# Sliding attention moved between the input projections of the first block, with an output projection by halves of rows and norm sums with tokens on partitions

## The chip, the cores and the metric

The kernel runs on one core of a Trainium2 chip. The metric is the device time of one execution in microseconds. The core has TensorE (PE in the rows, its weight loads PEld), VectorE (DVE), ScalarE (ACT), GpSimd (POOL) and SyncE (SP). They work through instruction streams of their own and meet at semaphores.

## The reference

Three transformer blocks on 256 tokens of width 1024 in float32. The change touches the mixer of the first one:

```python
mod = c_act @ w_ada[l] + b_ada[l]
shift1, scale1, gate1, shift2, scale2, gate2 = jnp.split(mod, 6, axis=-1)
h = modulate(x, norm1_g[l], shift1, scale1)
proj = h @ w_in[l]
q_g, k_g, v_g, a_lr, r_g, q_s, k_s, v_s = jnp.split(proj, split_at, axis=-1)
...
o_gla = rms_norm(o_gla, gla_norm_g[l].reshape(GLA_HEADS, GLA_DV)).reshape(bsz, s, GLA_WIDTH)
o_gla = o_gla * jax.nn.silu(r_g)
o_swa = swa_mixer(...)
o_swa = rms_norm(o_swa, swa_norm_g[l])
y = jnp.concatenate([o_gla, o_swa], axis=-1) @ w_out[l]
x = x + gate1[:, None, :] * y
h2 = modulate(x, norm2_g[l], shift2, scale2)
x = x + gate2[:, None, :] * peer_mixer(h2, ...)
```

`gla_mixer` is a gated linear attention in chunks of 64 tokens with 4 heads. `swa_mixer` is attention over a window of 128 keys with 8 query heads, 2 key heads and a sink logit per head. `peer_mixer` picks 16 of 128 x 128 experts per head and token. Two more blocks follow, with a sparse and a compressed attention; the change leaves them alone.

## The kernel before, in words

Everything is kept transposed: features on the 128 partitions, the 256 tokens along the row, a vector of width 1024 as 8 chunks. Weights come from HBM as 488 slots of 128x1024 float32 through a ring of four, in one fixed order (`_COUNTS`); SyncE refills a ring place as soon as `slots_used` says that it is free. Each engine's order is written out by hand in its block, and a projection result passes through one of two banks of `pu` (`entry`), freed by `evacs`.

*Front.* GpSimd issues 16 DMAs for the first rows of `w_ada` (the modulation). VectorE takes the dot product of each row with silu(c) (`modulation`), the squares of x are summed over features by matmuls with an all-ones matrix (`norm_sum`), which leaves the same sum in all 128 partitions, ScalarE takes the root, VectorE the reciprocal of 128x256, and scales x into `HTf`. Before the reciprocal VectorE waits for six small DMAs (`small_loaded`) to copy a table of position biases, which TensorE spreads in eight matmuls (line 724). A low-rank product (line 729) gives the gate logits.

*Projections.* 18 slots of `w_in` in the order qg, kg, rg, qs, ks, vg, vs; the first 13 by `project` (line 555, 8 matmuls of 256 columns), five by `project_tokens` (line 567, 16 of 128). ScalarE copies each result out (rg through Silu). A float32 matmul is two passes in the trace. Beside them VectorE takes the cumulated gates and 18 of the remaining 32 modulation rows, which come through a ring of four rows (`aring`) that GpSimd refills in a loop (line 444), one row for each row used.

*Gla.* After the last projection ScalarE makes five exponentials, VectorE seven products (lines 1690 to 1695), and TensorE scores (line 755), transposes, states, inner and outer products (to line 788). The norm over each head's 128 features sums into `pm` and `pn` and takes the reciprocal of 128x1024 (line 1730).

*Sliding attention.* `attend("swa", ...)` has 16 units, one per head and block of 128 tokens: the 8 of the first block have 128 keys, the others 256. In step u, TensorE does the scores of unit u (line 666) into one of four banks, the transposition of unit u-3 (line 675) and the products of unit u-4 (line 702); VectorE adds bias, takes the maximum and normalizes, ScalarE exponentiates and copies. Eight modulation rows are fillers of VectorE there. Then comes its norm, again through `norm_sum`.

*Output projection.* Each of 8 slots of `w_out` gives 128 output features from all 8 chunks of the input (`up_slot`). Products here and later are made of three passes (`three`, lines 587 to 589), with the weights and the input split into a high and a low part: ScalarE writes `ring_hi` (line 368), VectorE or GpSimd subtracts to get `ring_lo` (line 375); the same for the input, `Xh` and `Xl` (`x_high`, `x_low`). VectorE adds the residual. ScalarE squares each chunk, GpSimd adds the squares (`h2sum`).

*Second norm and peer query.* Root, reciprocal, scaling, high and low parts of eight chunks (lines 1804, 1810), then 16 slots of `peer_q`, whose low parts are GpSimd's; after each, `key_scores` (line 842) and VectorE's selection of the best 16. GpSimd fills most of the large buffer `big` with ones for a later stage: its middle, where gla's tensors lay (`mid_lo` to `mid_hi`, line 449, after `gla_done`), and the rest (lines 451 and 452). `aring` lies in `big` too. From here on, 128 slots of `peer_u` and all that follows are the same in both kernels.

## Time and profile before

| | |
|---|---|
| median of 3 runs | 1766.5 us (1765.46 to 1768.02) |
| profiled execution | 1767.21 us, span 1765.6 us |
| PE busy | 1650.5 us, 93% of the span |
| DVE, ACT, POOL busy | 1078.7, 855.1, 487.9 us |
| granted TensorE clock, mean | 0.951 |

The span runs from the first to the last instruction of the profiled execution. Busy shares are means over stages that have different limits, so what one stage costs is read from stretches of the timeline. The granted clock is a share of 2.4 GHz and has two levels, 0.5 and 1.0; a value between is a mean over time.

### The profile page before, as it was taken

To read this page: it belongs to the slowest core of one execution; us is meant where nothing else is said; L and a number is where in the kernel's file an instruction comes from. 1 tells how busy PE (TensorE), PEld (TensorE's weight loads), DVE (VectorE), ACT (ScalarE), POOL (GpSimd) and SP (SyncE) were. 2 spreads that over 40 slices of the span, in tenths; PEclk is the share of its full clock that TensorE was granted. 3 is DMA by queue.
4 is the path that set the end of the run, shared out by engine and by line. 5 is a ranking of instruction groups with operands and counts; after the bars stand their busy time and mean duration, and the time that the engine had idled before them with its cause. 6 is when DMAs were issued, how large, how long until landed. Compare 5 with 4: busy or idle time off the path is not lost.

```text
span 1765.6 us, 33664 instructions
## 1 busy us (share of the span) xinstructions
PE 1650.5 (93%) x11072; PEld 1492.8 (85%) x11072; DVE 1078.7 (61%) x2455; ACT 855.1 (48%) x1808; POOL 487.9 (28%) x465
## 2 busy tenths in 40 slices
PE   5975889998999999999999999889999998899998
PEld 2773689998999999987888887779999988789997
DVE  5536558953777771355555555866555665755555
ACT  3213445555454444555555554265555535654554
POOL 3110456986666668500000001320000000310000
PEclk8985699999999999999999999889999999999999
DMA  8861144554443445555555555215555456045554
GB/s 309 312 226 57 39 138 144 170 178 140 143 140 134 142 143 169 182 192 192 192 190 190 190 190 178 78 58 165 181 181 185 147 176 205 25 144 175 185 187 155
DMA packets 81329, 288.17 MB, mean 163 GB/s; under 512 B 10144, under 2 KB 11472, under 8 KB 81136
## 3 DMA queue, kind: packets, MB, share of 16 engines
q1 hardware_dynamic: 72448, 257.30, 44.6%
q0 software_dynamic: 7488, 26.87, 4.1%
q10 hardware_dynamic: 1328, 3.15, 0.5%
q8 instruction: 39, 0.64, 0.1%
q14 instruction: 26, 0.21, 0.0%
HBM read 284.66 MB, written 2.62 MB: 163 GB/s over the span
## 4 chain that ended last, share of the span: by engine, by line
PE 83%; DVE 8%; ACT 3%; issue 2%; DMA 2%; POOL 1%; SPq 0%; DVEq 0%; ACTq 0%; POOLq 0%
PE pu L587 12%; PE pu L588 12%; PE pu L589 12%; PE pacc L646 8%; PE pacc L644 8%; PE pacc L645 8%; PE pu L555 3%; PE pu L567 2%; PE pacc L587 2%; PE pacc L589 2%; PE pacc L588 2%; PE pacc L702 2%; PE pm L874 2%; PE pn L874 2%; DVE ring_lo L375 1%
## 5 line engine op out<-in xcount | busy, mean ns | idle before, releaser
L368 ACT ACTIVATE ring_hi<-ring 128x512 fp32r<-128x512 f32 x912 | 524.2, 622 | 546.7 <-PE pu L589 290.5
L375 DVE TENSOR_TENSOR ring_lo<-ring,ring_hi 128x512 fp32r<-128x512 f32 x624 | 407.4, 695 | 356.5 <-ACT ring_hi L368 356.1
L587 PE MATMUL pu<-Xh,ring_hi 128*128 128x256 f32 x1472 | 432.5, 294 | 21.6 <-DVE stats L1756 4.3
L588 PE MATMUL pu<-Xl,ring_hi 128*128 128x256 f32 x1472 | 420.1, 285 | 0.0
L589 PE MATMUL pu<-Xh,ring_lo 128*128 128x256 f32 x1472 | 420.0, 285 | 0.0
L375 POOL TENSOR_TENSOR ring_lo<-ring,ring_hi 128x512 fp32r<-128x512 f32 x288 | 370.3, 1307 | 131.4 <-ACT ring_hi L368 130.8
L587 PEld LDWEIGHTS pu<-Xh,ring_hi 128*128 128x128 f32 x1472 | 285.9, 194 | 28.8 <-issue 15.7
L588 PEld LDWEIGHTS pu<-Xl,ring_hi 128*128 128x128 f32 x1472 | 286.5, 195 | 0.2
L589 PEld LDWEIGHTS pu<-Xh,ring_lo 128*128 128x128 f32 x1472 | 285.8, 194 | 0.0
L644 PE MATMUL pacc<-ring_hi,vh 128*128 128x512 f32 x512 | 200.5, 392 | 0.0
L646 PE MATMUL pacc<-ring_lo,vh 128*128 128x512 f32 x512 | 200.5, 392 | 0.0
L645 PE MATMUL pacc<-ring_hi,vl 128*128 128x512 f32 x512 | 199.8, 390 | 0.0
L587 PE MATMUL pu<-X2h,ring_hi 128*128 128x256 f32 x512 | 146.3, 286 | 3.2 <-DVE big L2088 3.2
L589 PE MATMUL pu<-X2h,ring_lo 128*128 128x256 f32 x512 | 145.6, 284 | 0.0
L588 PE MATMUL pu<-X2l,ring_hi 128*128 128x256 f32 x512 | 145.6, 284 | 0.0
L644 PEld LDWEIGHTS pacc<-ring_hi,vh 128*128 128x128 f32 x512 | 96.0, 187 | 33.2 <-issue 5.6
L646 PEld LDWEIGHTS pacc<-ring_lo,vh 128*128 128x128 f32 x512 | 96.1, 188 | 21.0
L645 PEld LDWEIGHTS pacc<-ring_hi,vl 128*128 128x128 f32 x512 | 96.2, 188 | 16.0
L473 POOL DMA_DIRECT2D big<-bias_row x8 | 4.3, 549 | 363.1 <-DVE stats L1999 363.1
L587 PEld LDWEIGHTS pu<-X2h,ring_hi 128*128 128x128 f32 x512 | 99.0, 193 | 4.2 <-DVE big L2088 3.6
L588 PEld LDWEIGHTS pu<-X2l,ring_hi 128*128 128x128 f32 x512 | 98.9, 193 | 0.3
L589 PEld LDWEIGHTS pu<-X2h,ring_lo 128*128 128x128 f32 x512 | 99.0, 193 | 0.0
(390 smaller groups left out, 2653.1 us busy)
## 6 DMA issues: line engine op xcount, KB each, us to landing
ring<-in_weights SPq DMA_DIRECT2D x488, 512.0 KB, 3.3
big<-in_ada POOLq DMA_DIRECT2D x40, 512.0 KB, 6.7
bias_row<-big ACTq DMA_DIRECT2D x1, 1536.0 KB, 6.9
XT<-in_xT ACTq DMA_DIRECT2D x1, 1024.0 KB, 8.2
scr<-in_ada POOLq DMA_DIRECT2D x2, 512.0 KB, 12.3
tk<-in_ada POOLq DMA_DIRECT2D x2, 512.0 KB, 14.0
early_h<-in_ada POOLq DMA_DIRECT2D x2, 512.0 KB, 16.0
early_l<-in_ada POOLq DMA_DIRECT2D x2, 512.0 KB, 17.6
```

Of the source, the lines that this page charges most:

```text
L368: nc.scalar.activation(ring_hi[:, n % 2, half], ring[:, n % RING, half], ACT.Copy).then_inc(s["split_hi"], 1)
L375: api.tensor_tensor(ring_lo[:, n % RING, half], ring[:, n % RING, half], ring_hi[:, n % 2, half], ALU.subtract).then_inc(s[LOW[name][0]], 1)
L555: last = mm(entry(e), slot(n)[:, c * P:(c + 1) * P], rhs[:, c, :], start=(c == 0), stop=(c == C - 1))
L567: last = mm(entry(e)[:, tt * P:(tt + 1) * P], lhs[:, c, tt * P:(tt + 1) * P], slot(n)[:, c * P:(c + 1) * P], start=(c == 0), stop=(c == C ...
L587: mm(out, ring_hi[:, n % 2, w], xh, start=start, stop=False, skip_group_check=True)
L588: mm(out, ring_hi[:, n % 2, w], xl, start=False, stop=False, skip_group_check=True)
L589: return mm(out, ring_lo[:, n % RING, w], xh, start=False, stop=stop, skip_group_check=True)
L644: mm(out, xh[:, rows], ring_hi[:, n % 2, w], start=False, stop=False, skip_group_check=True)
L645: mm(out, xl[:, rows], ring_hi[:, n % 2, w], start=False, stop=False, skip_group_check=True)
L646: last = mm(out, xh[:, rows], ring_lo[:, n % RING, w], start=False, stop=False, skip_group_check=True)
L702: last = mm(out, v, p, start=(kind != "nsa" and k == 0 and UNITS[u][4]), stop=(k == len(pairs) - 1 and UNITS[u][5]), skip_group_check=(kin ...
L874: last = mm((pm, pn)[k % 2][:, i * P:(i + 1) * P], sq[:, j // 2, j % 2 * P:(j % 2 + 1) * P], scr[:, j * P:(j + 1) * P], start=True, stop=True)
```

## The change

- *Order of the weights.* `w_in` comes as qs, ks, vs, qg, kg, vg, rg. `w_out` comes as four slots for the attention's 512 input features and four for gla's; each slot gives 256 output features from four input chunks (`halves_of`, `out_slot`), so each output chunk gets two residuals, and each residual has two halves.
- *Attention among projections.* `attend` may return one step as a function. After projection 6 + k, TensorE does the steps that `steps_after(k, 20)` names, one or two. ScalarE follows the same table after each copy out. Scores use two banks (`pm`, `pn`) in place of four. VectorE's fillers there are one modulation row per step and, from step 8, the seven gla products. The gla exponentials stand after copy 5 on ScalarE. Silu of rg is one operation later on.
- *Sums with tokens on partitions.* For the norms of the input, the attention and gla, the squares are the stationary operand and one column of ones moves, so 128 tokens come out as a column of 128 partitions. Root and reciprocal are 128x2 or 128x8. A matmul of the column, repeated 128 times (`over_columns`), with the identity spreads it over all partitions again (`spreads`), and VectorE reads it from PSUM. The second norm keeps the old form.
- *Waits.* The bias table has a semaphore for its own two DMAs (`relb_loaded`). GpSimd's two long memsets become 14 of at most 128x1024, one after each low part of `peer_q`; ahead of the first low part GpSimd waits for `ada_used` to reach 48, all rows. VectorE takes modulation rows 40 to 43 in the output projection and 44 to 47 after the second norm.

```diff
+EARLY, BESIDE = 6, 12
...
+def steps_after(k, total):
+
+    return range(k * total // BESIDE, (k + 1) * total // BESIDE)
+
+
+NORMS = ["n1", "swa", "gla", "n2", "fin", "attn0", "lat", "mlp0", "attn1", "mlp1", "fin2"]
...
+        def over_columns(col):
+
+            return bass.AP(tensor=col.tensor, offset=col.offset, ap=[list(col.ap[0]), [0, P]])
+
+        def score_psum(u, banks=4):
+            return (pm[:, 0:T], pn[:, 0:T], pu[:, 0, 0:T], pu[:, 1, 0:T])[u % banks]
...
-            for dst, src, sem in ((cols[:, :], cols_d, "cols_loaded"), (relb[0:NB, :], relb_d, "small_loaded"),
-                                  (oneh[0:NB, :], onehot_d, "small_loaded"), (walr, small_d[:, :, 0:16], "small_loaded"),
+            for dst, src, sem in ((cols[:, :], cols_d, "cols_loaded"), (relb[0:NB, :], relb_d, "relb_loaded"),
+                                  (oneh[0:NB, :], onehot_d, "relb_loaded"), (walr, small_d[:, :, 0:16], "small_loaded"),
...
-            pool.wait_ge(s["x_split"], 2 * XSPLIT["w_out"] + 2)
-            step(nc.gpsimd.memset(big[:, GATED_FROM:mid_lo, :], 1.0))
-            nc.gpsimd.memset(big[:, mid_hi:NKEY, :], 1.0).then_inc(s["ones_set"], 1)
...
-            for c in range(2, C - 1):
...
             last.then_inc(s["h2_sum"], 1)
             pool.wait_ge(s["slots_used"], SLOT["peer_q"])
+            pool.wait_ge(s["x_split"], 2 * XSPLIT["w_out"] + 2)
+            pool.wait_ge(s["ada_used"], MOD)
+            parts = [(k, min(k + 4, hi)) for lo, hi in ((GATED_FROM, mid_lo), (mid_hi, NKEY)) for k in range(lo, hi, 4)]
             for i in range(2 * PH):
                 split_low(pool, nc.gpsimd, "peer_q", i)
+                for lo, hi in parts[i::2 * PH]:
+                    step(nc.gpsimd.memset(big[:, lo:hi, :], 1.0))
+            nc.gpsimd.memset(ones_flag, 1.0).then_inc(s["ones_set"], 1)
...
+                banks = 2 if kind == "swa" else 4
...
                 def scores(u):
-                    if u >= 4:
-                        pe.wait_ge(s["att_biased"], u - 3)
-                    mm(score_psum(u)[:, 0:keys_of(u)], query(u), keys(u), start=True, stop=True)\
+                    if u >= banks:
+                        pe.wait_ge(s["att_biased"], u + 1 - banks)
+                    mm(score_psum(u, banks)[:, 0:keys_of(u)], query(u), keys(u), start=True, stop=True)\
                         .then_inc(s["att_scored"], 1)
...
-            norm_sum("n1")
-            pe.wait_ge(s["small_loaded"], 16 * 6)
+            pe.wait_ge(s["squares"], SQUARED["n1"])
+            for tt in range(TT):
+                for c in range(C):
+                    last = mm(pn[:, tt:tt + 1], sq[:, c, tt * P:(tt + 1) * P], ones[:, 0:1], start=(c == 0), stop=(c == C - 1))
+            last.then_inc(s["sums"], 1)
+            pe.wait_ge(s["consts_made"], 1)
+            pe.wait_ge(s["inverses"], 1)
+            for tt in range(TT):
+                last = mm(pm[:, tt * P:(tt + 1) * P], over_columns(R[:, tt:tt + 1]), ident[:, :], start=True, stop=True)
+            last.then_inc(s["spreads"], 1)
+            pe.wait_ge(s["relb_loaded"], 16 * 2)
...
+            for i in range(18):
+                if i == 5 or 10 <= i < 14:
+                    project_tokens(SLOT["w_in"] + i, USE["w_in"] + i, HTf)
+                else:
+                    project(SLOT["w_in"] + i, USE["w_in"] + i, HTf)
...
+                if i == EARLY:
+                    pe.wait_ge(s["la_parts"], 1)
+                    pe.wait_ge(s["evacs"], USE["w_in"] + EARLY)
+                if i >= EARLY:
+                    for step in steps_after(i - EARLY, swa_steps):
+                        swa_step(SPAN["swa"][0] + step)
...
+            pe.wait_ge(s["squares"], SQUARED["swa"])
+            for tt in range(TT):
+                for c in range(4):
+                    last = mm(paccf[:, tt:tt + 1], sq[:, c, tt * P:(tt + 1) * P], ones[:, 0:1], start=(c == 0), stop=(c == 3))
+            last.then_inc(s["sums"], 1)
...
+            pe.wait_ge(s["inverses"], 2)
+            for tt in range(TT):
+                last = mm(paccf[:, tt * P:(tt + 1) * P], over_columns(R[:, tt:tt + 1]), ident[:, :], start=True, stop=True)
+            last.then_inc(s["spreads"], 1)
...
+            def out_slot(i):
...
+                pe.wait_ge(s["evacs"], e - 1)
+                if i % 4 == 0:
+                    pe.wait_ge(s["x_split"], 2 * XSPLIT["w_out"] + i // 4 + 1)
+                for j in range(2):
+                    for c in range(4):
+                        if j == 0 and c % 2 == 0:
+                            split_ready("w_out", i, c // 2, None)
+                        last = three(pu[:, e % 2, j * T:(j + 1) * T], n, slice(c * T + j * P, c * T + (j + 1) * P),
+                                     Xh[:, x0 + c, :], Xl[:, x0 + c, :], c == 0, c == 3)
+                last.then_inc(s["slots_used"], 1)
...
+            out_slot(0)
...
-            for i in range(C):
-                up_slot("w_out", i, USE["w_out"] + i, None, 0, "w_out" if i == 0 else None)
...
+            for h in range(GH):
+                for tt in range(TT):
+                    last = mm(paccf[:, h * TT + tt:h * TT + tt + 1], sq[:, h, tt * P:(tt + 1) * P], ones[:, 0:1], start=True, stop=True)
+            last.then_inc(s["sums"], 1)
+            out_slot(1)
+            pe.wait_ge(s["inverses"], 3)
+            for h in range(GH):
+                for tt in range(TT):
+                    col = 8 + h * TT + tt
+                    last = mm((pm, pn)[h // 2][:, (h % 2 * TT + tt) * P:(h % 2 * TT + tt + 1) * P], over_columns(R[:, col:col + 1]),
+                              ident[:, :], start=True, stop=True)
+            last.then_inc(s["spreads"], 1)
+            for i in range(2, 8):
+                out_slot(i)
+
...
+            act.wait_ge(s["sums"], NORM["n1"])
+            f(R[:, 0:TT], pn[:, 0:TT], ACT.Sqrt, scale=1.0 / D, bias=eps[:, 0:1]).then_inc(s["roots"], 1)
...
+                    evac(n_slot, rs[:, i - 14, :], src)
+                if i == EARLY - 1:
+                    act.wait_ge(s["ex_ready"], 1)
+                    inv = 1.0 / GATE_TEMP
...
+                    act.wait_ge(s["row_stored"], 16)
+                if i >= EARLY:
+                    for st in steps_after(i - EARLY, swa_steps):
+                        swa_step(SPAN["swa"][0] + st)
+            swa_step(SPAN["swa"][1] + 4)
...
+            squares(os_, sq[:, 0:4, :])
...
+            act.wait_ge(s["sums"], NORM["swa"])
+            f(R[:, 0:TT], paccf[:, 0:TT], ACT.Sqrt, scale=1.0 / 512, bias=eps[:, 0:1]).then_inc(s["roots"], 1)
+            split_high(act, "w_out", 0)
...
+            split_high(act, "w_out", 1)
+            act.wait_ge(s["evacs"], USE["w_in"] + 18)
+            f(rs, rs, ACT.Silu).then_inc(s["silu_done"], 1)
+            act.wait_ge(s["normed"], NORM["swa"])
+            x_high(os_, 0)
...
+            x_high(og, 1)
+            for i in range(3, 6):
...
+            for i in range(4, C - 1):
+                if i + 2 < C:
+                    split_high(act, "w_out", i + 2)
+                else:
+                    split_high(act, "peer_q", i + 2 - C)
+                act.wait_ge(s["evacs"], USE["w_out"] + i + 1)
+                for c in (2 * i - 8, 2 * i - 7):
+                    f(sq[:, c, :], XT[:, c, :], ACT.Square).then_inc(s["h2_sq"], 1)
...
-            dve.wait_ge(s["small_loaded"], 16 * 6)
-            v.tensor_copy(relb_all[0:NB, :, :], strided(relb[0:NB, 0:1], [[1, NH], [0, P]])).then_inc(s["relb_spread"], 1)
+            modulation(0, 4)
             dve.wait_ge(s["roots"], NORM["n1"])
-            step(v.reciprocal(R[:, 0:T], R[:, 0:T]))
+            v.reciprocal(R[:, 0:TT], R[:, 0:TT]).then_inc(s["inverses"], 1)
+            modulation(4, 2)
+            dve.wait_ge(s["spreads"], 1)
             for c in range(C):
-                last = v.scalar_tensor_tensor(HTf[:, c, :], XT[:, c, :], column("n1", c), R[:, 0:T], ALU.mult, ALU.mult)
+                last = v.scalar_tensor_tensor(HTf[:, c, :], XT[:, c, :], column("n1", c), pm[:, 0:T], ALU.mult, ALU.mult)
...
+            modulation(2 * C, 6)
...
+            def swa_filler(i):
+
+                modulation(2 * C + 6 + i, 1)
+                if 8 <= i < 8 + 3 + NSUB:
+                    gla_product(i - 8)
+
+            dve.wait_ge(s["consts_made"], 1)
+            dve.wait_ge(s["small_loaded"], 16 * 4)
+            attend("swa", swa_bias, filler=swa_filler)
...
+            for i in range(4):
+                last = v.scalar_tensor_tensor(os_[:, i, :], os_[:, i, :], column("swa_g", i), paccf[:, 0:T], ALU.mult, ALU.mult)
+            last.then_inc(s["normed"], 1)
+            split_low(dve, v, "w_out", 0)
...
+            x_low("w_out", os_, 0)
+            split_low(dve, v, "w_out", 1)
+            dve.wait_ge(s["ada_used"], 2 * C + 24)
+            step(v.tensor_tensor(mod[:, 16:40], mod[:, 16:40], cols[:, COL["b_ada"] + 16:COL["b_ada"] + 40], ALU.add))
+            step(v.tensor_scalar(gain[:, 8:16], mod[:, 32:40], 1.0, None, ALU.add))
+            step(v.tensor_tensor(gain[:, 8:16], gain[:, 8:16], cols[:, COL["n2"]:COL["n2"] + 8], ALU.mult))
+            modulation(2 * C + 24, 1)
...
+            v.reciprocal(R[:, 8:8 + GH * TT], R[:, 8:8 + GH * TT]).then_inc(s["inverses"], 1)
...
+            def out_residual(i):
+
+                e = USE["w_out"] + i
+                dve.wait_ge(s["slots_used"], SLOT["w_out"] + i + 1)
+                for j in range(2):
+                    o = 2 * (i % 4) + j
+                    last = v.scalar_tensor_tensor(XT[:, o, :], pu[:, e % 2, j * T:(j + 1) * T], mod[:, 16 + o:17 + o], XT[:, o, :],
+                                                  ALU.mult, ALU.add)
+                last.then_inc(s["evacs"], 1)
...
+            out_residual(0)
+            modulation(2 * C + 25, 1)
+            dve.wait_ge(s["spreads"], 3)
...
+            dve.wait_ge(s["silu_done"], 1)
             v.tensor_tensor(og, og, rs, ALU.mult).then_inc(s["gla_done"], 1)
...
+            split_low(dve, v, "w_out", 2)
+            out_residual(1)
+            x_low("w_out", og, 1)
+            for i in range(2, C):
+                if i + 1 < C:
+                    split_low(dve, v, "w_out", i + 1)
+                out_residual(i)
+                if i < 4:
+                    modulation(2 * C + 24 + i, 1)
+            rest = 2 * C + 28
...
+            modulation(rest, MOD - rest)
+            dve.wait_ge(s["ada_used"], MOD)
+            step(v.tensor_tensor(mod[:, 40:48], mod[:, 40:48], cols[:, COL["b_ada"] + 40:COL["b_ada"] + 48], ALU.add))
...
-        tiles(np.concatenate([qg, kg, rg, qs, ks, vg, vs], axis=1)), tiles(w_out),
+        tiles(np.concatenate([qs, ks, vs, qg, kg, vg, rg], axis=1)), halves_of(w_out[512:]), halves_of(w_out[:512]),
```

The order of TensorE among the projections (`pu` holds projections, `pm` and `pn` scores, `pacc` transpositions and products; L555, L567 and from now L571, L583 are projections). Before:

```order
L555 MATMUL pu<-big,ring 128x256 x8
L737 MATMUL pn<-big 128x256 x2
L555 MATMUL pu<-big,ring 128x256 x96
L567 MATMUL pu<-ring,big 128x128 x80
L755 MATMUL pm<-big 64x16 x16
```

With the change, from projections 1 to 4 on:

```order
L571 MATMUL pu<-big,ring 128x256 x32
L583 MATMUL pu<-ring,big 128x128 x16
L571 MATMUL pu<-big,ring 128x256 x8
L684 MATMUL pm<-big 128x128
L571 MATMUL pu<-big,ring 128x256 x8
L684 MATMUL pn<-big 128x128
L684 MATMUL pm<-big 128x128
L571 MATMUL pu<-big,ring 128x256 x8
L684 MATMUL pn<-big 128x128
L693 MATMUL pacc<-ident,big 128x128
L684 MATMUL pm<-big 128x128
L693 MATMUL pacc<-ident,big 128x128
```

One or two units' pieces now stand behind each projection, and the gla scores (L755) come behind all of them.

The order of GpSimd from the loop of modulation rows to the low parts of the peer query, with the semaphores it waits on. Before:

```order
L444 DMA big<-in_ada 128x1024
L440 REGISTER_ALU
L440 COMPARE_AND_BRANCH
L449 MEMSET big 128x1024 [waits gla_done]
L449 MEMSET big 128x1024 [waits chain_pool] x7
L449 MEMSET big 128x512 [waits chain_pool]
L451 MEMSET big 128x5632 [waits x_split,chain_pool]
L452 MEMSET big 128x8192 [waits chain_pool]
L455 TENSOR_TENSOR R<-sq 128x256 [waits h2_sq]
L458 TENSOR_TENSOR R<-R,sq 128x256 [waits h2_sq,chain_pool] x5
L375 TENSOR_TENSOR ring_lo<-ring,ring_hi 128x512 [waits split_hi,slots_used]
L375 TENSOR_TENSOR ring_lo<-ring,ring_hi 128x512 [waits split_hi] x31
```

With the change:

```order
L462 MEMSET big 128x1024 [waits gla_done]
L462 MEMSET big 128x1024 [waits chain_pool] x7
L462 MEMSET big 128x512 [waits chain_pool]
L465 TENSOR_TENSOR R<-sq 128x256 [waits h2_sq,chain_pool]
L468 TENSOR_TENSOR R<-R,sq 128x256 [waits h2_sq,chain_pool] x4
L388 TENSOR_TENSOR ring_lo<-ring,ring_hi 128x512 [waits ada_used,split_hi,x_split,slots_used]
L388 TENSOR_TENSOR ring_lo<-ring,ring_hi 128x512 [waits split_hi]
L479 MEMSET big 128x1024
L388 TENSOR_TENSOR ring_lo<-ring,ring_hi 128x512 [waits split_hi,chain_pool]
```

The long memsets are gone from ahead of the sum of squares, a piece stands behind each two halves of a low part, and the first low part has `ada_used` among its waits.

## Rows read from the trace of the kernel before

**Rows 1.** Busy time by stretches: start:end and length, PE, PEld, DVE, ACT, POOL busy, clock, DMA.
```profile
42.10:112.40 70.30, 67.55 (x373) 60.11 (x372) 28.75 (x46) 13.33 (x27) 9.52 (x18) 0.95 0.83 309
112.40:122.06 9.66, 0.00 (x1) 0.01 (x1) 4.36 (x8) 5.24 (x7) 0.00 (x0) 0.76 0.18 54
122.06:140.03 17.97, 17.28 (x212) 16.51 (x212) 9.30 (x19) 1.68 (x3) 3.17 (x6) 0.50 0.53 177
...
147.55:163.50 15.95, 1.23 (x8) 0.93 (x8) 14.65 (x20) 5.39 (x10) 0.00 (x0) 0.50 0.00 0
163.50:197.60 34.10, 32.83 (x96) 17.19 (x96) 27.55 (x91) 15.68 (x61) 10.34 (x13) 0.52 0.19 62
...
206.80:232.90 26.10, 26.10 (x193) 25.91 (x194) 12.51 (x20) 11.73 (x22) 16.14 (x8) 0.88 0.45 138
232.90:244.90 12.00, 6.54 (x28) 5.03 (x26) 9.24 (x20) 5.89 (x12) 4.93 (x4) 0.72 0.17 54
248.70:295.00 46.30, 46.30 (x393) 46.30 (x392) 34.81 (x204) 22.25 (x54) 33.23 (x27) 1.00 0.48 160
```

**Rows 2.** Timeline of ScalarE in the projections: start, us, what [idle before <-releaser].
```profile
84.17 0.38 ACT L1168 ACTIVATE big<-pu 128x256 f32<-128x256 f32 x1 [3.07 <-PE pu L555]
```

**Rows 3.** Chain of waits, first 160 us: start, length, piece.
```profile
5.91 16.66 DMA sinks<-in_sinks
22.60 0.68 DVE big L1647
23.28 1.67 DVE R L1649
24.98 3.25 DVE big L1651 x8
...
147.55 6.57 DVE big L1730
```

**Rows 4.** Timelines of ScalarE and VectorE: the first root, a modulation row, an attention bias.
```profile
17.07 0.47 ACT L1168 ACTIVATE R<-pn,eps 128x256 f32<-128x256 f32 x1 [4.20 <-PE pn L577]
...
18.14 1.22 DVE L1638 CUSTOM_DVE_ANT_0 scr<-scr,big 128x1024 f32<-128x1024 f32 x1
...
184.95 0.41 DVE L1743 SCALAR_TENSOR_TENSOR big<-big,pn 128x256 f32<-128x256 f32 x1
```

**Rows 5.** Waits from 240 to 480 us: who waited for whom, total, times, longest.
```profile
DVE scr L1896 <- ACT tk L1168: 43.6, 1, 43.6
```

**Rows 6.** Chain of waits in the sliding attention, a unit with 256 keys.
```profile
183.69 1.15 PE pn L666 x2
184.84 0.62 PE pacc L675 x2
185.46 1.05 PE pacc L702 x4
```

**Rows 7.** The last block's attention: TensorE's timeline, and the stretch (columns as rows 1).
```profile
1520.23 0.27 PE L675 MATMUL pacc<-ident,big 128*128 128x128 f32 x1
1520.34 0.61 PE L702 MATMUL pacc<-big 128*128 128x128 f32 x4
...
1521.22 0.27 PE L675 MATMUL pacc<-ident,big 128*128 128x128 f32 x1
...
1520.00:1525.00 5.00, 5.00 (x37) 4.36 (x36) 4.23 (x16) 4.13 (x18) 2.38 (x5) 1.00 0.01 3
```

**Rows 8.** The same view as rows 1: the first 6.3 us of the output projection.
```profile
206.80:213.10 6.30, 6.30 (x30) 6.30 (x31) 1.28 (x2) 1.75 (x3) 3.89 (x1) 0.51 0.00 0
```

**Rows 9.** Timeline of GpSimd: memsets, and low parts of the peer query's weights.
```profile
175.27 8.69 POOL L449 MEMSET big<- 128x1024 f32 x9
...
233.11 4.93 POOL L375 TENSOR_TENSOR ring_lo<-ring,ring_hi 128x512 fp32r<-128x512 f32 x4 [0.52 <-PE pu L589]
```

**Rows 10.** Chain of waits in the second norm: the root.
```profile
235.37 0.48 ACT R L1168
```

205 lines of the change are left out of this document (91 added, 114 removed).

## Prediction

> **What bounds the kernel now.** I read four views of the trace before: the busy time by stretches, the chain of waits, the timelines of single engines, and the waits. The stretches [rows 1] show two kinds of stage. In the input projections (42.1 to 112.4 us), the output projection (206.8 to 232.9) and everything from 248.7 on, TensorE is busy throughout; each projection tile takes 3.45 us (0.38 of ScalarE's copy and 3.07 of its wait), a little more in the token form [rows 2]. Between 112.4 and 206.8 us TensorE either idles or works at a granted clock of about 0.5, the 1.2 GHz level. It waits 9.7 us for exponentials and gla products, works 18.0 us on gla, idles nearly all of 147.6 to 163.5, then spends 34.1 us on sliding attention. In the chain [rows 3] a reciprocal of 128x1024 alone costs 6.57 us. At the front, the chain runs through the DMA of the sinks into a small copy at 22.60, and only then to the reciprocal for the first norm, though the root was ready at 17.54 [rows 4]. So what the change moves lies on the path to the end, up to the first peer query; behind that TensorE is the bound, and VectorE, which would be late next, sits 43.6 us waiting on ScalarE [rows 5]. A gain at the front should therefore reach the end whole.
>
> **The change, part by part.** I follow the kernel by the moments at which stages begin. All differences are after minus before.
>
> 1. Front. The copy of the bias table now waits for its own two small DMAs, and the sums with tokens on partitions make the reciprocal 128x2 instead of 1.67 us wide. The two dot products that end at 19.4, 1.22 each [rows 4], become the last thing ahead of the scaling, which starts at 19.6 instead of 24.98 [rows 3]. All later modulation rows were there without a wait, so the first projection moves from 42.1 to 36.7: **-5.4** (bounds -3, if late rows of DMA hold it, and -6).
>
> 2. Projections and attention together. TensorE's own work adds up. At the half clock a unit with 256 keys is 1.15 + 0.62 + 1.05 = 2.8 us [rows 6], and the whole stage 34.1 [rows 1]. The attention of the last block does the same kind of steps at clock 1.00: a step of one transposition, four products and a 256-wide score repeats every 0.99 us [rows 7]. At those rates (0.11 per 128-wide pass, 0.22 per 256-wide one) eight short units are 8 x 0.56 and eight long ones 8 x 1.11, together 13.4. Half of 34.1 is 17. I take **+16** (bounds 13.4, and 20 with small waits). Cover: a step needs 2.2 us of VectorE for 128 keys and 3.1 for 256 keys (0.41 of bias, about as much of maximum, 0.5 of reciprocal and scaling, 0.1 of copy, 1.22 of a modulation row [rows 4], 0.6 of a gla product), while TensorE, with 12 projections and 16 us over 20 steps, comes round every 2.9 us. VectorE thus holds the pace, with little to spare in the second half. ScalarE's five gla exponentials (5.2 us busy with their table load, [rows 1]) lie beside projections 6 and 7.
>
> 3. The gap of 9.7 us ahead of the gla scores goes, for gla's products are done in VectorE's fillers: **-9.7**.
>
> 4. Gla. Before: 18.0 us at clock 0.50. Added are 16 one-column passes for the attention's sums and 4 passes that spread the roots, 2.5 us at 0.11 to 0.13 each; a gain is that the stage now follows dense work, so its first few us should run at the full clock. I take 17.5: **-0.5** (bounds -9, all of it at full clock, and +3).
>
> 5. From the last gla product to the end of the output projection. Before: 140.0 to 232.9 is 92.9 us. After, counted from that product: VectorE adds (1.0), ScalarE has Silu's table load and 1.1 for x_high, x_low takes 1.2, so slot 0 starts at 2.9. Its 24 passes run at the half clock, 6.30 us for 30 [rows 8], to 8.1; sums 1.5; slot 1 2.9; the gla spread 16 x 0.11, to 14.8. Then TensorE has nothing: four scalings 1.7, the product with rs 1.2 and the first half of slot 2's low part 0.6 stand ahead, to 18.4. Slots 3, 4 and 5 start each 3.2 apart, since VectorE puts two half splits (1.2), two residuals (0.8) and a modulation row or x_low (1.2) between them; slots 5, 6 and 7 take 2.9 each. End: 36.7. Difference **-56.1** (bounds -60 and -51).
>
> 6. The second norm. Before: 12.0. The last residual is two outputs wide (+0.8 with its square). GpSimd is now late: it leaves its loop of modulation DMAs only when row 43 is used, 27.4 in the count of step 5, then does nine memsets in 8.7 us [rows 9] and five additions of 0.8, so its sum arrives 4.0 after the last slot. Three matmuls, 1.7 in all, then the old 9.5 from root to last low part (235.4 to 244.9) [rows 1, 10]: 15.2, **+3.2** (bounds 0.8 and 5).
>
> 7. The wait for all modulation rows. The freed region holds the ring of rows, so GpSimd may not start peer_q's low parts before row 47 is used, and VectorE uses the last four after the norm: 4 x 1.15 = 4.6. Queued behind that wait are the low parts of slots 0 and 1, which before were done at 233 to 238, ahead of need [rows 9]. TensorE starts 1.3 after the rows, 5.9 from the norm's end, on a cold clock: slot 0 5.1, slot 1 3.4, scores 0.45, so slot 2 begins 14.8 after the norm instead of 3.8: **+11.0** (bounds 5, at full clock, and 14).
>
> 8. Memsets among the splits. Each of 14 slots of peer_q gets 0.9 more on GpSimd: 2.5 (4.93 for two slots) + 0.95 = 3.5 against TensorE's 3.3, the 46.3 us of 14 slots [rows 1, 9]. That loses 0.2 a slot, 2.5 in all, and the low parts are about as far ahead: **0** (bounds 0 and +4). The two long memsets that they replace were off the path and return nothing. VectorE's selection may be slowed by them, and is covered by its 43.6 us.
>
> Sum: -5.4 + 16 - 9.7 - 0.5 - 56.1 + 3.2 + 11.0 = **-41.5 us**. The profiled execution took 1767.2 us (span 1765.6), the median is 1766.5, 0.7 lower. 1766.5 - 41.5 = **1725 us**.
>
> **Rivals.**
> A. *The clock falls among the projections* (slower). Each burst of attention has short waits and transpositions. If TensorE's clock goes to 0.5 at project 7 and stays, 12 tiles go from 3.45 to 6.8 each (+40) and attention from 16 to 34 (+18): 1725 + 58 = 1783 us. The result changes sign when the half clock holds over some 41 of these 58, 70% of the stage. For it: the old attention kept TensorE busy for 32.8 of 34.1 us, and the granted clock was 0.52 in the mean [rows 1]. Against it: the last block's attention stood at 1.00, as from 1520 to 1525 [rows 7], and here dense tiles lie between the bursts. I give 5%. The Trainium skill, in "TensorE: Matmul & The Clock Gate", section "A second HAM failure mode: psum-queue depth-cycling", says that short idle moments between matmul groups that cycle through PSUM banks are frequent enough to make the clock swing between its levels; this kernel now cycles two score banks. By that rule the sum would lie near this rival, or halfway to it; by the row of the last block the clock stays. The row decides for me.
> B. *The attention's chain is exposed at every step.* With two score banks in place of four, a step waits on the bias of the one before the last, and VectorE's 3.1 us in the second half may exceed TensorE's round. Ten steps late by 1 us give +10, 1735 us; chains exposed by 1.5 us in all 16 units give +24, 1749 us. For it: VectorE's 3.1 against 2.9. Against it: units lie one whole projection apart. 15%.
> C. *Gla and slot 0 at the full clock*, since dense work goes ahead: -9 and -2, 1714 us. Against it: gla ran at 0.50 through 64-wide products and never raised the clock [rows 1]. 12%.
> D. *Little of it shows*, because VectorE or GpSimd, not TensorE, ends what comes after (peer_q at GpSimd's 3.5 or worse, the selection past its 43.6 us): +15 to +40, up to 1765 us. 5%.
>
> **How the numbers follow.** My forecast, the sum with its sizes off by up to 10, gets 63%; A 5%, B 15%, C 12%, D 5%. The range leaves out A, D and the far part of B: **1712 to 1745 us**. No change within 0.2% (3.5 us, about what these runs can tell) is only an edge of D and of A's partial form: 1%. Slower: A, 4%. Faster: 95%.
>
> **What would show it.** In the profile after: VectorE's first scaling near 19.6 us; the first projection near 37; clock 1.0 from 55 to 120 us, with attention's passes 0.11 and 0.22 long; gla scores starting near 123; output projection from about 143 to 177 with a hole of 3 to 4 us after slot 1; nine memsets ending near 177 and TensorE waiting on GpSimd's sum; VectorE's four dot products between the norm and GpSimd's first peer_q split, with TensorE idle for some 6 us there; then slots of peer_q at 3.3 to 3.5. Steps 2, 5 and 7 carry the sum: step 2 is wrong if the clock row falls among the projections, 5 if slots 2 to 7 take over 22 us, 7 if the first peer query starts without GpSimd's wait.

## The result, and the profile after

The changed kernel takes **1737.6 us** (median of 4 runs, 1736.7 to 1738.2) against 1766.3 for the kernel before beside it (4 runs, 1765.5 to 1768.0): a ratio of 0.985, 95% interval 0.983 to 0.987, or 28.7 us less. 1725 was forecast, 1712 to 1745 was the range. The profiled execution took 1736.7 us (span 1735.0, granted clock 0.971 in the mean; before 1765.6 and 0.951).

The stretches of the trace after answer to [rows 1]. The cuts are the starts of the scaling, of the first projection, of project 6, of the gla scores, of the second part of gla, the end of gla, slot 0 of the output projection and its end, root and end of the second norm, the first peer query and its slot 2. Columns as there.

```profile
21.31:38.39 17.08, 15.16 (x33) 6.01 (x31) 15.74 (x39) 8.07 (x16) 2.13 (x4) 1.00 0.87 333
38.39:65.15 26.76, 24.04 (x117) 20.53 (x117) 12.71 (x20) 7.46 (x13) 2.64 (x5) 0.94 0.72 261
65.15:129.91 64.76, 64.42 (x363) 50.24 (x361) 43.93 (x125) 26.64 (x82) 10.05 (x19) 1.00 0.80 278
129.91:134.40 4.49, 4.49 (x130) 4.46 (x129) 0.00 (x0) 1.33 (x2) 0.00 (x0) 1.00 0.28 103
134.40:148.30 13.90, 13.89 (x105) 13.02 (x104) 5.42 (x14) 7.50 (x11) 0.00 (x0) 0.51 0.00 1
148.30:150.75 2.45, 0.00 (x0) 0.03 (x1) 2.35 (x4) 2.43 (x4) 0.00 (x0) 0.50 0.00 0
...
165.99:185.16 19.17, 19.14 (x144) 18.66 (x144) 14.87 (x28) 9.10 (x19) 9.03 (x11) 0.93 0.56 192
185.16:192.45 7.29, 2.90 (x7) 1.85 (x6) 1.03 (x3) 1.67 (x4) 3.81 (x6) 0.79 0.20 75
192.45:201.82 9.37, 0.00 (x0) 0.00 (x0) 8.47 (x18) 4.42 (x9) 0.00 (x0) 0.68 0.00 1
201.82:207.88 6.06, 0.00 (x0) 0.03 (x1) 4.79 (x10) 0.00 (x0) 1.36 (x2) 0.50 0.00 0
207.88:216.43 8.55, 8.55 (x53) 8.55 (x53) 0.00 (x0) 1.53 (x4) 7.63 (x7) 0.69 0.18 61
216.43:266.05 49.62, 48.51 (x399) 47.50 (x397) 36.96 (x218) 24.25 (x59) 43.61 (x41) 1.00 0.47 156
```

The hole ahead of the gla scores, the idle stretch behind gla and the 34 us of attention at half clock [rows 1] are gone. TensorE is busy for 64.42 of the 64.76 us of projections with attention, at clock 1.00 throughout. TensorE still idles 4.35 us for GpSimd's sum ahead of the second norm, 9.4 through the norm and 6.1 more until the first peer query. With the stage starts of both traces, each step of the prediction can be measured:

| step | forecast | measured | from |
|---|---|---|---|
| 1 front | -5.4 | -3.7 | first projection 42.1, now 38.39 |
| 2 projections with attention | +16 | +21.2 | 70.3 (42.1 to 112.4), now 91.5 (38.39 to 129.91) |
| 3 gap before gla | -9.7 | -9.7 | 9.66, now none |
| 4 gla | -0.5 | +0.4 | 17.97, now 18.39 |
| 5 to the end of the output projection | -56.1 | -56.0 | 92.9, now 36.9 |
| 6 second norm | +3.2 | +4.7 | 12.0, now 16.7 |
| 7 peer query head | +11.0 | +10.8 | 3.8, now 14.6 |
| 8 memsets among the splits | 0 | +1.1 | slot 2 to the first peer_u low part: 48.5, now 49.6 |

Together -31.2 where the spans differ by 30.6; the medians differ by 28.7, since the profiled execution before was 0.9 over its median and that after 0.9 under it. Half of what is missing from the forecast lies in step 2.

One part of such differences is chance. From the first projection to project 6 this profile took 26.8 us and that of changed_again, the same kernel, 25.2. In both TensorE idles 2.7 us for ScalarE there; the granted clock then fell in the one (0.72 in the mean from 50 to 55 us) and stayed at 1.00 in the other. From project 6 to the gla scores both took 64.8 us. So differences of single stages are firmer than those of whole profiles.

The timeline of TensorE in one burst of two units with 128 keys, between two projection tiles (start, us, operation):

```profile
83.24 3.84 PE L583 MATMUL pu<-ring,big 128*128 128x128 f32 x32
87.01 0.48 PE L684 MATMUL pm<-big 64*128 64x128 f32 x2
87.42 0.33 PE L693 MATMUL pacc<-ident,big 128*128 128x128 f32 x1
87.68 0.43 PE L720 MATMUL pacc<-big 128*64 128x128 f32 x2
88.04 0.48 PE L684 MATMUL pn<-big 64*128 64x128 f32 x2
...
89.08 3.84 PE L583 MATMUL pu<-ring,big 128*128 128x128 f32 x32
```

No idle time stands in these rows, yet a unit takes 1.04 us from score to score; five passes at 0.11 would be 0.55. A long unit takes 1.57 instead of 1.11. The tile behind a burst takes 0.2 longer (83.24 to 87.01, 3.77; a tile in this form behind another takes 3.57). The score works on 64 rows of the array, the transposition on 128 by 128, the products on 64 columns. In the last block all are 128 by 128, and there a unit took what its passes take [rows 7].

A small tile is not slow in itself. Once two units' scores stand directly behind each other, on the two halves of the rows:

```profile
72.77 0.37 PE L684 MATMUL pn<-big 64*128 64x128 f32 x1
72.77 0.37 PE L684 MATMUL pm<-big 64*128 64x128 f32 x1
72.98 0.27 PE L684 MATMUL pn<-big 64*128 64x128 f32 x1
72.99 0.27 PE L684 MATMUL pm<-big 64*128 64x128 f32 x1
73.19 3.72 PE L571 MATMUL pu<-big,ring 128*128 128x256 f32 x16
```

Their four passes overlap and take 0.42 us together (72.77 to 73.19), no more than the two passes of one score (87.01 to 87.42).

### The profile page after: what moved, and what is told of

Same layout as the page of the kernel before. It is cut to its first block, busy times and chain, and to the rows that moved or that the text cites. A ratio compares the mean times of both kernels' runs of the same rounds, so it can differ in the third digit from the quotient of the medians.

```text
span 1735.0 us, 33824 instructions
## 1 busy us (share of the span) xinstructions
PE 1641.3 (95%) x11134; PEld 1493.5 (86%) x11134; DVE 1067.8 (62%) x2463; ACT 852.9 (49%) x1806; POOL 487.2 (28%) x477
## 4 chain that ended last, share of the span: by engine, by line
PE 81%; DVE 8%; POOL 4%; issue 3%; ACT 3%; DMA 1%; DVEq 0%; ACTq 0%; POOLq 0%; SPq 0%
PE pu L603 12%; PE pu L604 11%; PE pu L605 11%; PE pacc L660 8%; PE pacc L662 8%; PE pacc L661 8%; POOL ring_lo L388 3%; PE pu L571 3%; PE pu L583 2%; PE pacc L604 2%; PE pacc L603 2%; PE pacc L605 2%; PE pn L948 2%; PE pm L948 2%; PE pacc L720 1%
## 5 line engine op out<-in xcount | busy, mean ns | idle before, releaser
L662 PEld LDWEIGHTS pacc<-ring_lo,vh 128*128 128x128 f32 x512 | 96.1, 188 | 21.2
```

What stands on the lines that cost most here:

```text
L662: last = mm(out, xh[:, rows], ring_lo[:, n % RING, w], start=False, stop=False, skip_group_check=True)
```

## Experiments

The chip of each group ran the kernel before as well; differences to the changed kernel are taken from the ratios to it (the changed kernel's own, measured again: 0.9851). Of the three chips only that of combined, scores_only and old_norm ran the changed kernel too; for the other runs its ratio stands in. "By the trace" means between profiled executions.

| run | median, us | ratio to before, 95% | less than the changed kernel |
|---|---|---|---|
| changed_again | 1737.0 | 0.9851 (0.9833 to 0.9869) | |
| full_tiles | 1729.0 | 0.9815 (0.9802 to 0.9829) | 6.3 |
| rows_early | 1728.3 | 0.9812 (0.9798 to 0.9825) | 6.9 |
| sum_first | 1730.9 | 0.9825 (0.9812 to 0.9839) | 4.6 |
| behind | 1759.9 | 0.9987 (0.9975 to 0.9999) | -24.0 |
| combined | 1721.0 | 0.9755 (0.9737 to 0.9773) | 16.9 |
| order_alone | 1723.1 | 0.9777 (0.9756 to 0.9797) | 13.1 |
| combined2 | 1718.0 | 0.9746 (0.9728 to 0.9763) | 18.5 |

The last column is uncertain by 4 to 5 us, from the intervals of both ratios; the rows from traces are finer.

**changed_again.** The changed kernel as it stands.

> The changed kernel itself, run beside the kernel before on the chip of the three that follow, so that they can be compared with it there. Both theories: 0.983 to 0.987 of the kernel before.

**full_tiles.** Scores on 128 rows, products on 128 columns; the unwanted half is zero (keys) or not copied out (products).

```diff
-                    evac(n_slot, ks, src)
+                    f(kz[0:64, 0, :], src[0:64, :], ACT.Copy)
+                    f(kz[64:P, 1, :], src[64:P, :], ACT.Copy).then_inc(s["evacs"], 1)
...
-                return qs[half_rows(u), h % 4, tt * P:(tt + 1) * P]
+                return qs[:, h % 4, tt * P:(tt + 1) * P]
-                return ks[half_rows(u), 0:keys_of(u)]
+                return kz[:, u % 2, 0:keys_of(u)]
-                r = half_rows(u)
-                return r, [vs[:, k, r] for k in range(TT)]
+                return slice(0, P), [vs[:, k, :] for k in range(TT)]
```

> Sliding attention on TensorE with whole 128x128 tiles: the scores take all 128 partitions (the keys stand in a copy whose other half is zero), the products take all 128 columns of the values (the half that is not wanted is not copied out). The number of passes is the same as in the changed kernel. Theory S, the excess of step 2 is a fixed cost each time that TensorE goes between tiles of 64 rows, 128 rows and 64 columns: a short unit falls from 1.04 to about 0.56 us and a long one from 1.57 to about 1.1, the 0.2 us that each tile behind a burst loses comes back, the gla scores start near 119.5 instead of 129.9, and the time is 8 to 10 us below the changed kernel's 1737.6. Theory W, the excess is waiting of each piece on semaphores and on the piece before it: units stay at 1.04 and 1.57, the time within 1 us of 1737.6.

TensorE's timeline of full_tiles, two short units and one long one:

```profile
83.27 0.39 PE L685 MATMUL pm<-big 128*128 128x128 f32 x2
83.50 0.27 PE L694 MATMUL pacc<-ident,big 128*128 128x128 f32 x1
83.61 0.39 PE L721 MATMUL pacc<-big 128*128 128x128 f32 x2
83.83 0.39 PE L685 MATMUL pn<-big 128*128 128x128 f32 x2
84.05 0.27 PE L694 MATMUL pacc<-ident,big 128*128 128x128 f32 x1
84.53 0.46 PE L721 MATMUL pacc<-big 128*128 128x128 f32 x2 [0.20 <-ACT big L1243]
...
103.58 0.59 PE L685 MATMUL pn<-big 128*128 128x256 f32 x2
...
104.67 0.60 PE L685 MATMUL pm<-big 128*128 128x256 f32 x2
```

Units of 0.56 and 1.09 us, tiles of 3.46 and 3.57 behind bursts. The stage from project 6 to the gla scores takes 57.50 us (63.47 to 120.97) instead of 64.76. By the ratios the run is 6.3 us faster, 4 either way, so that all of the 7.3 may reach the end. Theory S holds: the same number of passes costs 7.3 us less once the tile's shape does not change. W, waits on semaphores and dependencies, is excluded as the main cost, for the steps' waits are the same. A part of W appears only now: some products wait 0.2 to 0.5 us for ScalarE's copy, as at 84.53, about 2.4 us in all (bursts sum to 15.5 us, their passes to 13.1), which is why 7.3 was gained and not 10.

**scores_only.** The edits above without the last, that of the products' values.

> Of the whole tiles only the scores are kept (128 rows, keys padded with zeros); the products again write 64 columns. It tells whether the cost lies in going between row shapes, column shapes, or both. If both cost alike, about 0.15 to 0.2 for each passage: the score behind a projection 0.22 instead of 0.42, transposition 0.11 instead of 0.26, the products still 0.36, and the piece behind them (score or projection) longer by up to 0.2: a burst of one short unit takes 0.7 to 0.9. If only the rows matter: 0.55 as with whole tiles. If only the columns: 1.04 as in the changed kernel.

```profile
84.77 0.49 PE L685 MATMUL pn<-big 128*128 128x128 f32 x2
85.10 0.27 PE L694 MATMUL pacc<-ident,big 128*128 128x128 f32 x1
85.30 0.43 PE L721 MATMUL pacc<-big 128*64 128x128 f32 x2
85.66 3.84 PE L584 MATMUL pu<-ring,big 128*128 128x128 f32 x32
```

A unit behind another takes 0.89 us (0.33, 0.20, 0.36), a tile behind it 3.67 in the token form; the stage 60.62 (63.71 to 124.33). So both shapes cost: rows 4.1 of the 7.3 us, columns 3.1. The transposition before the products also lengthens (0.20, not 0.11), so the cost falls on the piece before a passage as well as on the one behind it. One execution took 1731.9 us.

**behind.** All twenty steps behind the last projection.

```diff
-    return range(k * total // BESIDE, (k + 1) * total // BESIDE)
+    return range(total) if k == BESIDE - 1 else range(0)
```

> All twenty attention steps come behind the last input projection instead of between the projections; every instruction is the same. Theory, between projections only TensorE's own work of the attention costs time, and alone the pace of VectorE (2.2 us for a short unit and 3.1 for a long one, with its modulation row and its gla product) would be exposed, 42 us for 16 units instead of TensorE's 22: slower than the changed kernel by 15 to 25 us, and the granted clock falls to 0.5 behind the projections. Rival, the attention costs about its 22 us wherever it stands: within 4 us of the changed kernel.

Timeline of TensorE in the second half of behind:

```profile
133.78 1.22 PE L684 MATMUL pn<-big 64*128 64x256 f32 x2 [0.17 <-DVE big L1802]
134.93 0.69 PE L693 MATMUL pacc<-ident,big 128*128 128x128 f32 x2
135.55 1.11 PE L720 MATMUL pacc<-big 128*64 128x128 f32 x4
136.83 1.22 PE L684 MATMUL pm<-big 64*128 64x256 f32 x2 [0.17 <-DVE big L1802]
```

The stretch of its attention (columns as in the first block above):

```profile
107.00:151.30 44.30, 35.81 (x105) 18.61 (x104) 41.99 (x123) 16.68 (x64) 9.01 (x17) 0.54 0.65 200
```

Steps with 256 keys come 3.05 us apart, VectorE is busy for 41.99 of 44.30 us, and the granted clock of the stretch is 0.54, near the 1.2 GHz level. TensorE's own pieces there take 2.88 of the 3.05 us at that clock, so VectorE's pace is the limit by little. The gla scores start at 151.3 instead of 129.9, and the run is 24.0 us above the changed kernel. Interleaving is thus what makes the attention cheap: 44.3 us alone, 22.9 between the projections. It also contains what rival A feared: with the attention alone the clock does fall; between dense tiles it stayed at 1.00. The number of banks does not tell the two apart: the kernel before, with four, stood at 0.52 [rows 1].

**rows_early.** VectorE's last four dot products ahead of its wait for the root.

```diff
             v.tensor_copy(stats[:, 0:1], stats[:, 0:1]).then_inc(s["x_ready"], 1)
+            modulation(rest, MOD - rest)
             dve.wait_ge(s["roots"], NORM["n2"])
...
             h2_low(C - 1)
-            modulation(rest, MOD - rest)
```

> VectorE takes the last four modulation rows between the last residual and its wait for the root of the second norm, instead of behind the norm. Theory of step 7, the wait for all modulation rows holds GpSimd's low parts and through them the first peer queries: GpSimd starts them at about 190 instead of 206.5, slot 2 of the peer queries starts 5 to 7 us after the second norm instead of 15.0, and the time falls by 8 to 10 us. Rival, the start of the peer queries is held by the cold clock of TensorE and the order of ScalarE's high parts: slot 2 still starts over 11 us after the norm, and at most 4 us are gained.

Timelines of rows_early, VectorE's dot products and GpSimd beside them:

```profile
185.77 1.22 DVE L1730 CUSTOM_DVE_ANT_0 big<-big 128x1024 f32<-128x1024 f32 x1
...
186.91 1.74 DVE L1730 CUSTOM_DVE_ANT_0 big<-big 128x1024 f32<-128x1024 f32 x1
...
185.82 6.73 POOL L468 TENSOR_TENSOR R<-R,sq 128x256 f32<-128x256 f32 x4
192.52 2.49 POOL L388 TENSOR_TENSOR ring_lo<-ring,ring_hi 128x512 fp32r<-128x512 f32 x2
```

GpSimd starts its low parts at 192.5 instead of 206.5, and slot 2 of the peer queries starts 3.7 us behind the norm instead of 14.6. But 6.9 us were gained and not 8 to 10, for a reason that neither text named: VectorE's dot products and GpSimd's additions slowed each other. Three of four dot products took 1.74 instead of 1.22, the four additions 6.73 instead of 3.13, and the root came 3.2 us later (195.64, with the output projection ending 0.4 earlier, at 184.75). The term of step 7 was right; its remedy had a price.

**sum_first.** The memsets of the middle region behind the additions.

```diff
-            for k in range(mid_lo, mid_hi, 4):
-                step(nc.gpsimd.memset(big[:, k:min(k + 4, mid_hi), :], 1.0))
             pool.wait_ge(s["h2_sq"], 2)
...
             last.then_inc(s["h2_sum"], 1)
+            for k in range(mid_lo, mid_hi, 4):
+                step(nc.gpsimd.memset(big[:, k:min(k + 4, mid_hi), :], 1.0))
```

> GpSimd's nine memsets of the middle region move from ahead of its additions for the second norm to behind them. Theory of step 6, the memsets make its sum late: TensorE's wait of 4.35 us ahead of the last sums falls under 1 us, the second norm starts 3 to 4 us earlier, nothing else moves since GpSimd then idles until 206.5, and the time falls by 3 to 4 us. Rival, memsets beside VectorE's scalings of the norm slow these down: those get longer by 10% or more and half of the gain is given back.

GpSimd's timeline in sum_first, where the output projection ends at 187.84:

```profile
186.66 1.54 POOL L465 TENSOR_TENSOR R<-R,sq 128x256 f32<-128x256 f32 x2 [1.05 <-ACT sq L1242]
188.14 8.59 POOL L471 MEMSET big<- 128x1024 f32 x9
```

The root follows the output projection's end by 2.98 us instead of 7.29: 4.3 us, near the 4.0 of step 6. The 4.6 by the ratios says the same, but is hardly clear of its own uncertainty. The scalings kept their 0.48 us beside the memsets; the rival falls.

**combined.** full_tiles, sum_first, and the four dot products one by one: behind the residuals of slots 5 and 6, and two behind the last.

```diff
+                elif i in (5, 6):
+                    modulation(2 * C + 23 + i, 1)
...
+            modulation(rest + 2, 2)
             dve.wait_ge(s["roots"], NORM["n2"])
```

> The attention with whole tiles, GpSimd's memsets behind its sum, and the last four modulation rows earlier: one each behind the residuals of slots 5 and 6, two behind the last residual, so that none stands beside GpSimd's additions for long and none delays the reciprocal. Theory that the three costs are separate, and that the two-sided slowing of dot product and addition (1.22 to 1.74, 3.13 to 6.73) took back 3.2 us from the early rows: from the end of the output projection to the first peer query 7.5 us instead of 22.7, then 0.5 more for a first query paced by the norm, and 7.3 less in the attention: 22 us below the changed kernel. Rival, the dot products make slots 6 and 7 of the output projection late, or still meet the additions: 16 to 19 us below.

```profile
175.83 2.37 DVE L389 TENSOR_TENSOR ring_lo<-ring,ring_hi 128x512 fp32r<-128x512 f32 x2
...
181.46 8.60 POOL L472 MEMSET big<- 128x1024 f32 x9
190.14 4.65 POOL L389 TENSOR_TENSOR ring_lo<-ring,ring_hi 128x512 fp32r<-128x512 f32 x2
```

16.9 us, the rival's 16 to 19, though mostly for a reason that it did not name. From the output projection's end to the first peer query 12.8 us passed instead of 7.5. The nine memsets now stood ahead of the first low part, which then ran beside the norm's scalings and took 4.65 instead of 2.5 us. The part that the rival named was smaller: VectorE's split of slot 7 met GpSimd's additions, 2.37 instead of 1.28.

**order_alone.** GpSimd's order alone: the low parts of slots 0 and 1 right behind the sum, the wait for the last row only ahead of the first memset over the ring of rows. VectorE unchanged.

```diff
             last.then_inc(s["h2_sum"], 1)
             pool.wait_ge(s["slots_used"], SLOT["peer_q"])
+            split_low(pool, nc.gpsimd, "peer_q", 0)
+            split_low(pool, nc.gpsimd, "peer_q", 1)
+            fill(middle[3:])
...
+            for i in range(2, 2 * PH):
                 split_low(pool, nc.gpsimd, "peer_q", i)
+                if i == 2:
+                    pool.wait_ge(s["x_split"], 2 * XSPLIT["w_out"] + 2)
+                    pool.wait_ge(s["ada_used"], MOD)
+                fill(parts[i - 2::2 * PH - 2])
```

> The changed kernel with another order on GpSimd alone: it makes the low parts of the first two peer query slots right behind its additions and waits for the last modulation row only ahead of the first memset that covers the ring of rows; three of the nine middle memsets stand in the gaps between its additions, six behind the second low part. VectorE keeps its four dot products behind the norm. Theory of steps 6 and 7 together: the sum is no longer late (4 us) and the first peer query follows the norm chunk by chunk: from the end of the output projection to the start of slot 2, 17 to 19 us instead of 30 to 31, so 12 to 13 us below the changed kernel. Rival, the low parts beside the reciprocal and the scalings of the norm slow each other as the dot products and the additions did: 20 to 23 us for that stretch, 7 to 10 gained.

GpSimd and VectorE in order_alone:

```profile
184.37 4.95 POOL L388 TENSOR_TENSOR ring_lo<-ring,ring_hi 128x512 fp32r<-128x512 f32 x4
...
197.79 4.11 POOL L388 TENSOR_TENSOR ring_lo<-ring,ring_hi 128x512 fp32r<-128x512 f32 x2 [2.95 <-ACT ring_hi L381]
...
197.30 1.22 DVE L1740 CUSTOM_DVE_ANT_0 big<-big 128x1024 f32<-128x1024 f32 x1
198.45 2.31 DVE L1740 CUSTOM_DVE_ANT_0 big<-big 128x1024 f32<-128x1024 f32 x1
```

From the output projection's end (183.99) to the start of slot 2 (199.99) 16.0 us passed instead of 31.3 in the changed kernel, a little better than forecast; 3.0 of the 15.3 us are lost again in the slots behind (52.7 us from slot 2 to the first peer_u low part, not 49.6), where the low part of slot 2 meets the last two dot products (4.11 instead of 2.5, 2.31 instead of 1.22). 13.1 us less in all: with two waits ordered anew, steps 6 and 7 give back most of what they took.

**combined2.** order_alone and full_tiles.

> GpSimd's order as in the run order_alone, with the attention on whole tiles. Theory that the attention's gain (7.3 us by the traces, 6 to 8 by the medians) and the gain of that order are independent: 18 to 20 us below the changed kernel, 3 below the first combination. Rival, one hides part of the other: under 16.

18.5 us less than the changed kernel, within the theory's 18 to 20, and 1718.0 us is the lowest median of the study. Its stretch from the output projection's end to slot 2 is again 16.0 us (177.74 to 193.74). Against the first combination the difference (1.6 by the ratios) is within the noise.

**The front: old_norm, old_wait, mod_first.** One execution each, read from the trace. In this order, the core of each edit:

```diff
-            for tt in range(TT):
-                for c in range(C):
-                    last = mm(pn[:, tt:tt + 1], sq[:, c, tt * P:(tt + 1) * P], ones[:, 0:1], start=(c == 0), stop=(c == C - 1))
+            norm_sum("n1")
...
-            modulation(0, 4)
+            modulation(0, 6)
             dve.wait_ge(s["roots"], NORM["n1"])
-            v.reciprocal(R[:, 0:TT], R[:, 0:TT]).then_inc(s["inverses"], 1)
-            modulation(4, 2)
-            dve.wait_ge(s["spreads"], 1)
+            step(v.reciprocal(R[:, 0:T], R[:, 0:T]))
```

```diff
-            dve.wait_ge(s["relb_loaded"], 16 * 2)
-            v.tensor_copy(relb_all[0:NB, :, :], ...
             dve.wait_ge(s["c_silu"], 1)
             modulation(0, 4)
+            dve.wait_ge(s["relb_loaded"], 16 * 2)
+            dve.wait_ge(s["small_loaded"], 16 * 4)
+            v.tensor_copy(relb_all[0:NB, :, :], ...
```

```diff
-            modulation(0, 4)
+            modulation(0, 6)
             dve.wait_ge(s["roots"], NORM["n1"])
             v.reciprocal(R[:, 0:TT], R[:, 0:TT]).then_inc(s["inverses"], 1)
-            modulation(4, 2)
```

> The first norm again with sums over 128 rows and 256 tokens and a reciprocal of 128x256, but with the changed kernel's wait for the bias table. Theory, the gain at the front came from the wait and not from the small reciprocal: sums 5.3 us instead of 6.96, the root near 17.1 instead of 18.7, reciprocal 1.7 wide, no spread; the scaling starts at 20.7 to 21.3, as in the changed kernel (21.3) or earlier. Rival, the small reciprocal carries it: the scaling starts over 1 us later than 21.3.

> Of the front only the wait is undone: the copy of the bias table again waits for all six small DMAs and stands behind the first four dot products; the one-column sums and the 128x2 reciprocal stay. Theory, the front's gain is this wait: the copy ends near 22.7 as in the kernel before, reciprocal, two dot products and the scaling queue behind it, which starts at 25.2 instead of 21.3. Rival, the wait was covered: the scaling starts within 1 us of 21.3.

> Dot products 4 and 5 move from behind the first norm's reciprocal to ahead of it. In the changed kernel VectorE idles 2.16 us for the root and then has both dot products, 2.4 us, while the spread is ready after 1.5. Theory, the late root (one-column sums of 6.96 us) is now what binds the front: reciprocal at 19.2, scaling at 20.8 instead of 21.3. Rival, the rows 4 and 5 come late by DMA and then delay the reciprocal: scaling at 21.3 or later.

The sums and the scaling in the changed kernel, then in old_norm:

```profile
11.66 6.96 PE L745 MATMUL pn<-ones,sq 128*128 128x1 f32 x32 [11.66 <-ACT sq L1242]
...
18.66 0.26 ACT L1242 ACTIVATE R<-pn,eps 128x2 f32<-128x2 f32 x1 [5.84 <-PE pn L745]
...
21.31 3.22 DVE L1745 SCALAR_TENSOR_TENSOR big<-XT,cols,pm 128x256 f32<-128x256 f32 x8
```

```profile
11.63 5.51 PE L593 MATMUL pn<-sq,ones 128*128 128x256 f32 x16 [11.63 <-ACT sq L1234]
...
17.17 0.47 ACT L1234 ACTIVATE R<-pn,eps 128x256 f32<-128x256 f32 x1 [4.39 <-PE pn L593]
...
21.00 3.26 DVE L1735 SCALAR_TENSOR_TENSOR big<-XT,cols,R 128x256 f32<-128x256 f32 x8
```

old_wait's scaling starts at 25.61 behind a copy at 22.65, mod_first's at 20.90. So the wait carries the whole gain of the front (4.3 us); the new form of the first norm is worth nothing there (21.00 with the old one, 21.31 with the new), and the late root plus VectorE's order cost 0.4. The three executions took 1737.9, 1740.4 and 1737.0 us (old_norm, old_wait, mod_first); only old_wait's lies outside the changed kernel's nine, 1735.7 to 1738.2.

## Why the prediction was right or wrong

The forecast was right in direction, mechanism and range, and 12.6 us too low. That is further off than the 10 us which it allowed its own sizes. The room above came from rival B, whose mechanism did not occur, so that the range held is in part luck. All five steps that missed by 0.9 us or more (1, 2, 4, 6 and 8) came out slower than forecast.

- **Step 2, the term that was mis-sized.** "At those rates (0.11 per 128-wide pass, 0.22 per 256-wide one) ... together 13.4 ... I take +16" should have been 22.9 (64.76 less twelve tiles of 3.45 or 3.57, 41.9), outside the bounds of 13.4 to 20 that it gave. Of this 1.7 is hidden in the difference of the stages, mostly by a shorter fall of the clock near its start (ScalarE's third copy stands 17.9 us behind the first projection's start in the trace before, 16.5 now). The rates came from [rows 7], where all pieces use the whole array; the pieces here change the shape three times per unit, and each return to a projection costs 0.2. How far the clock falls there is chance: with the 25.2 us of changed_again the step would read +19.6. The runs full_tiles and scores_only showed the cost of the shapes: with one shape a unit takes 0.56 and 1.09, as the rates said. The cover was reckoned rightly: VectorE's pace of 3.1 us for 256 keys was 3.05 when exposed.
- **Step 1** was too large by 1.7: the wait went as said. The text left 0.2 us between the last dot product (19.4) and the scaling (19.6); in mod_first, which has that order, reciprocal and spread take 1.5 there (19.36 to 20.90). The edit moreover puts these dot products behind the reciprocal, and the one-column sums bring the root at 18.66, not near 17.1: 0.4 more.
- **Steps 3, 5 and 7** came out to 0.2 us: no gap before gla; 36.9 us from the last gla product to the end of the output projection, with slot 0 after 2.45 (2.9 forecast) and a hole of 3.7 (3.6) behind slot 1; slot 2 of the peer queries 14.6 behind the norm (14.8). Inside step 5 two misses cancel, which is luck. The terms named up to the hole add to 14.3 us, not 14.8, and it began at 14.0, so slot 2 started at 17.7 instead of 18.4. The first twelve of its passes then ran at 0.21 us each, the half clock, which the text left out: slot 3 started 4.2 later, not 3.2.
- **Step 4** was 0.9 short. The first 4.5 us of gla ran at clock 1.00, as hoped, but the sixteen one-column passes took 3.41 us, not 2.
- **Step 6** was 1.5 short: GpSimd's sum came 4.35 late (4.0 forecast), and the three sums behind the wait took 2.9 at a lower clock, not 1.7. sum_first confirms the mechanism.
- **Step 8**: GpSimd's slot is 3.51 against 3.32, and the lead of its low parts is used up near the end; 1.1 us, inside the bounds.
- **Rivals.** A did not happen: clock 1.00 for 64.76 us. The Trainium skill's rule in "TensorE: Matmul & The Clock Gate", section "A second HAM failure mode: psum-queue depth-cycling", by which PSUM bank cycling makes the clock swing, did not show between dense tiles. With the steps alone the clock did not swing but stood near its lower level, at 0.54 in the run behind and at 0.52 with four banks before. B would have given +10 to +24 by waits; the size came close (+6.9 over step 2's term) but not the mechanism, since TensorE idles 0.34 us in the stage. C happened for gla's scores alone. D did not.

## What to carry to other kernels

Price a matmul that uses part of the array by rows with the same change of shape around it, not by its passes: here every passage between 64-row, whole and 64-column tiles cost 0.1 to 0.2 us, and padding to whole tiles beat the smaller tiles although it computes twice as much. Put dependent, latency-bound work between dense tiles: the same instructions cost 22.9 us there and 44.3 alone. When a region is freed for reuse, wait for it ahead of the one instruction that writes it, not ahead of everything on that engine, and keep additions on GpSimd away from VectorE's two-input operations.
